# A transformer block on one core: the weight split of the seventh input chunk in halves and quarters, two small steps moved, and a new start address for the activations

## What is computed

```
hx = modulate(rmsnorm(x, norm1_g), mx[0], mx[1])       # mx = silu(c) @ ada_w + ada_b
hc = modulate(rmsnorm(ctx, norm1_g), mc[0], mc[1])     # mc = silu(c_ctx) @ ada_w + ada_b
ux = hx @ w_in
uc = hc @ w_in          # only the columns of the two forget gates and of the values are used
```

## Time and profile before

| | |
|---|---|
| median of 3 runs | 767.01 us |
| the profiled execution | 766.55 us |
| its span, first to last instruction | 764.7 us |
| PE busy | 738.8 us (97%) |
| DVE, ACT, POOL busy | 492.9, 360.9, 398.5 us |
| mean granted TensorE clock | 0.991 |

### The profile page before, as it was taken

One profiled execution on the slowest core, in us unless ns is written; L12 is line 12 of the kernel. 1 busy time (PEld: TensorE's weight loads), 2 busy tenths in 40 slices (PEclk: granted clock), 3 DMA queues, 4 the chain that ended last, 5 costly groups with the idle time before them and its releaser, 6 DMA issues.

```text
span 764.7 us, 14160 instructions
## 1 busy us (share of the span) xinstructions
PE 738.8 (97%) x5844; PEld 716.3 (94%) x5844; DVE 492.9 (64%) x905; ACT 360.9 (47%) x458; POOL 398.5 (52%) x223
## 2 busy tenths in 40 slices
PE   6887999999999989999999999999999999999998
PEld 3776889999999989999999999999999999999998
DVE  4886698369616559867777774457855656556553
ACT  6685333344434465555555546445554434334331
POOL 0775544347457957787887787766785300000000
PEclk9999999999999989999999999999999999999999
DMA  9993867436633546465554554443435564554511
GB/s 361 419 397 120 312 255 287 192 111 211 231 111 115 175 151 256 170 213 173 198 186 165 183 203 143 153 147 111 165 111 198 188 214 160 177 207 161 184 56 56
DMA packets 21089, 145.84 MB, mean 191 GB/s; under 512 B 2465, under 2 KB 2977, under 8 KB 3746
## 3 DMA queue, kind: packets, MB, share of 16 engines
q1 hardware_dynamic: 20880, 144.87, 52.0%
q10 hardware_dynamic: 146, 0.07, 0.0%
HBM read 143.88 MB, written 1.05 MB: 190 GB/s over the span
## 4 chain that ended last, share of the span: by engine, by line
PE 89%; DMA 3%; ACT 3%; DVE 2%; issue 1%; POOL 1%; DVEq 0%; ACTq 0%; POOLq 0%
PE bank L1433 24%; PE bank L1434 23%; PE bank L1435 23%; PE bank L1451 4%; DMA raw<-in_w_in 3%; PE CP L1435 2%; PE CP L1434 2%; PE CP L1433 2%; PE bank L1540 2%; POOL wlo L463 1%; ACT whi L490 1%; DVE GA L1136 1%; PE bank L1491 0%; PE CP L1465 0%; PE bank L1476 0%
## 5 line engine op out<-in xcount | busy, mean ns | idle before, releaser
L469 POOL TENSOR_TENSOR wlo<-raw,whi 128x512 fp32r<-128x512 f32 (+1 forms) x193 | 367.9, 1936 | 173.0 <-ACT whi L487 173.0
L487 ACT ACTIVATE whi<-raw 128x2048 fp32r<-128x2048 f32 x101 | 192.5, 1907 | 46.3 <-PE bank L1435 29.2
L1203 DVE SCALAR_TENSOR_TENSOR Y<-bank,vec,Y 128x189 f32<-128x189 f32 (+2 forms) x352 | 123.0, 423 | 43.8 <-ACT Y L738 43.8
L1433 PE MATMUL bank<-H2h,whi 128*128 128x256 f32 x352 | 100.0, 284 | 1.7 <-DVE H2l L1178 1.7
L1434 PE MATMUL bank<-H2l,whi 128*128 128x256 f32 x352 | 100.8, 286 | 0.0
L1435 PE MATMUL bank<-H2h,wlo 128*128 128x256 f32 x352 | 100.6, 286 | 0.0
L1433 PE MATMUL bank<-H1h,whi 128*128 128x256 f32 (+1 forms) x288 | 91.5, 318 | 9.0 <-ACT whi L487 5.7
L1435 PE MATMUL bank<-H1h,wlo 128*128 128x256 f32 (+1 forms) x288 | 89.7, 311 | 0.0
L1434 PE MATMUL bank<-H1l,whi 128*128 128x256 f32 (+1 forms) x288 | 89.4, 310 | 0.0
L863 DVE TENSOR_TENSOR wlo<-raw,whi 128x2048 fp32r<-128x2048 f32 x28 | 64.4, 2300 | 34.5 <-ACT whi L487 34.5
L1433 PE MATMUL bank<-H4h,whi 128*128 128x256 f32 x256 | 72.6, 283 | 0.0
(11 more groups left out here) (327 smaller groups left out, 1892.6 us busy)
## 6 DMA issues: line engine op xcount, KB each, us to landing
raw<-in_w_mlp SPq DMA_DIRECT2D x32, 1024.0 KB, 4.8
raw<-in_w_in SPq DMA_DIRECT2D x30, 1024.0 KB, 5.4
raw<-in_ffn_up SPq DMA_DIRECT2D x22, 1024.0 KB, 4.9
raw<-in_ada_hi SPq DMA_DIRECT2D x16, 1024.0 KB, 5.4
raw<-in_ffn_down SPq DMA_DIRECT2D x11, 1024.0 KB, 4.8
raw<-in_w_out SPq DMA_DIRECT2D x8, 1024.0 KB, 4.8
ada_s<-in_ada_s SPq DMA_DIRECT2D x4, 1024.0 KB, 17.7
ada_p<-in_ada_p SPq DMA_DIRECT2D x2, 1024.0 KB, 10.1
```

The source lines that it names most:

```text
L469: m = e.tensor_tensor(l[:, a:a + step], r[:, a:a + step], h[:, a:a + step].bitcast(F32), ALU.subtract)
L487: e.activation(whi[q % NHI][:, :], raw[n % NRAW][:, :], ACT.Copy).then_inc(s["w_hi"], 1)
L1203: e.scalar_tensor_tensor(o[:, r0:r1, c0:c1], z[:, r0 + dr:r1 + dr, c0 + dc:c1 + dc], cw[:, f, tap:tap + 1], o[:, r0:r1, c0:c1], ALU.mult, ...
L1433: e.matmul(out, h[:, col:col + P], xh, start=first, stop=False, skip_group_check=True)
```

## The change

- `FINE` is 7: chunk 6, the first forget chunk, is split in halves on ACT and in quarters on POOL like the chunks before it.
- ACT makes the two halves of chunk 6 earlier in its order: the first behind the context's tile 3, the second behind tile 5. Before, the whole chunk stood behind tile 7.
- DVE does the context's reciprocal behind the dot products of `ada_s` 2, not ahead of them.
- PE does all of chunk 3 and tiles 0 to 4 of chunk 4 ahead of the context's row products; tiles 5 to 7 of chunk 4 and chunk 5 follow them. For chunk 6 it waits half by half and quarter by quarter.
- The shared area begins at 124224 (the next multiple of 1024, plus 320), 352 bytes further on; modulo 1024 that is 320 instead of 992.

No instruction of computation is added but for one: chunk 6's one ACT copy becomes two of half the size. No DMA is added or moved.

```
-FINE = 6
+FINE = 7
...
-    base = cursor[0]
+    base = (cursor[0] + 1023) // 1024 * 1024 + 320
...
         input_high(1, range(2, 4))
+        first_high(6, 0)
         scales(1, 2, 22)
         input_high(1, (4, 5))
+        first_high(6, 1)
         scales(1, 3, 24)
         input_high(1, (6, 7))
-        high(6)
...
+        ada_rows("ada_s", 2, 1)
         reciprocal(2, 2, ("rms_in", 2), "rstd_in")
-        ada_rows("ada_s", 2, 1)
...
-        first(3, range(0, 5), b3)
+        first(3, range(0, 8), b3)
+        b4 = group("w_in", 4)
+        first(4, range(0, 5), b4)
         e.wait_ge(s["rstd_in"], 2)
         e.wait_ge(s["h1_mul"], 8)
         rows(bank[5][:, T:2 * T], [wide(2), wide(3)], "row_in")
-        first(3, range(5, 8), b3)
+        first(4, range(5, 8), b4)
+        first(5, range(0, 8), group("w_in", 5))
...
-            if i < 6:
-                first(i, range(0, 8), group("w_in", i))
-            elif i < 10:
-                h, l = weights("w_in", i)
+            if i < 10:
+                if i == 6:
+                    h, l = whi[i % NHI], wlo[i % NHI]
+                else:
+                    h, l = weights("w_in", i)
                 for j in range(2):
                     b = group("w_in", i, j)
                     for k in range(KT):
                         if (i, j) == (6, 0):
+                            e.wait_ge(s["w_hi"], hi_at[i] - 1 + k // 4)
+                            e.wait_ge(s["lo_pool"], 4 * i + k // 2 + 1)
```

More of the change, by code:

```diff
@@ L1584, in tensor @@
         hx, hl = H1h[:, 0, :, :], H1l[:, 0, :, :]
-        for i in range(4, 20):
-            if i < 6:
-                first(i, range(0, 8), group("w_in", i))
-            elif i < 10:
-                h, l = weights("w_in", i)
+        for i in range(6, 20):
+            if i < 10:
[3 more added lines that the diff above has]
+                    h, l = weights("w_in", i)
                 for j in range(2):
```

## The result

The kernel after takes **740.48 us** (median of 4 runs, 737.7 to 743.66) against 766.97 of the kernel before in the same rounds (4 runs, 766.56 to 767.05). The ratio is 0.966, with a 95% interval of 0.961 to 0.970. The two sets do not overlap; against the later one, with its own kernel before at 766.47, the gain is 20.2 us and not 26.5.

A forecast was written before the change was run, and what follows sets the result against it. PE bounds the kernel, busy 738.8 of 764.7 us. Order 2.85, wait 5.8, clock 1.45, less 0.6, give 9.5 us at chunk 6's end, 8.2 at chunk 7; address nothing: 758.8 us from 767.01, own range 757 to 760.5, overall 753.5 to 763.5.

The forecast's parts named there:

- The order around the row products and chunk 6 in halves: Steps at PE's early chunks: chunk 6 starts at 62.85, chunk 7 at 75.95 instead of 84.15, 8.2 us gained.
- 2.85 by the order, 5.8 by the wait: Split of the 9.5 us gained by chunk 6's end; 1.45 by the clock, less 0.6, complete it.
- The lead is kept: Chunks behind chunk 7: DVE and loads keep up, narrowest place 3.4 us at chunk 9, so the 8.2 us stay.
- Rival 1: Chunks 8 to 13: late DVE or raw-ring loads lose 2 to 6 of the 8.2 us, 761 to 765; chance 0.13.
- The clock at short waits: PE's waits of 0.6 us in chunk 6 and 1.2 us before chunk 7 leave the full clock.
- Rival 6: Clock falls at the wait before chunk 7: 1.45 us less gain, 760.2; chance 0.02.
- the rule of the Trainium skill: A matmul stream with waits can repeatedly drop to half clock; if chunk 7 began slow, gain 6.8 instead of 8.2 us.
- rival 2: Half clock behind 275 us, worth 2.6 us, shrinks or goes as waits move: 756.2 to 757.5; chance 0.12.
- The area's address: Every 256-column matmul streaming from the shared area: at most 12.8 us either way, taken as nothing.
- Rival 3: 256-column matmuls get faster by the area's address: up to 12.8 us more, 746 to 757; chance 0.11.
- the page that I named: Skill's SBUF page, Door 1: lines of 16 bytes, begun by both area positions, so the address price would be nothing.

The follow-up runs named there:

- order alone: Kernel after with the shared area back at 992 modulo 1024, so only the new order remains: 758.08 us, ratio 0.989.
- k1: Kernel after with the remainder of the fourth w_mlp1 chunk made by DVE instead of POOL: 735.31 us, ratio 0.960.
- k3: Kernel after unedited, run again later for the spread of its times: 746.25 us (745.3 to 750.75), ratio 0.976.
- halves alone: Kernel before with only chunk 6 in halves and quarters and its earlier place on ACT: 758.74 us, ratio 0.991.
- rows alone: Kernel before with only PE's new order around the row products and the later reciprocal: 767.00 us, ratio 1.0005.
- f3: Kernel after with the area at 128 modulo 1024, distance 0 from the weight tiles: slowest of all, 256-column matmuls at 120.0 ns.
- f4: Kernel after with the area at 448 modulo 1024, distance 320 from the weight tiles (64 modulo 256); total time not in the text.
- h1: Kernel after with the area at 992 and weight tiles at 800 modulo 1024, distance 192: fast; total time not in the text.
- h2: Kernel after with the area at 576 modulo 1024, distance 448 (192 modulo 256): profiled execution 746.88 us.
- h3: Kernel after with the area at 832 modulo 1024, distance 704 (192 modulo 512): profiled execution 740.38 us.
- g2: Kernel after with the area at 352 modulo 1024, 224 bytes from the weight tiles' residue; total time not in the text.
- f2: Kernel after with weight tiles at 192 and the area at 384 modulo 1024, distance 192 kept; total time not in the text.

## Why the prediction was right or wrong

**The order around the row products and chunk 6 in halves: right.** The trace of order alone (address as before) is the one to hold against the steps. Its ACT, POOL and PE:

```profile
58.62 1.05 ACT L490 ACTIVATE whi<-raw 128x1024 fp32r<-128x1024 f32 x1
...
68.22 0.60 ACT L587 ACTIVATE SG<-bank 128x512 f32<-128x512 f32 x1
68.72 1.91 ACT L487 ACTIVATE whi<-raw 128x2048 fp32r<-128x2048 f32 x1
```

```profile
62.55 2.55 POOL L463 TENSOR_TENSOR wlo<-raw,whi 128x512 fp32r<-128x512 f32 x2 [0.26 <-ACT whi L490]
70.70 10.04 POOL L469 TENSOR_TENSOR wlo<-raw,whi 128x512 fp32r<-128x512 f32 x8 [5.60 <-ACT whi L487]
```

```profile
54.49 0.61 PE L1440 MATMUL bank<-con,RC 128*128 128x128 f32 x4
...
62.87 0.39 PE L1434 MATMUL bank<-H1h,whi 128*128 128x512 f32 x1
...
68.87 0.50 PE L1434 MATMUL bank<-H1h,whi 128*128 128x512 f32 x1 [0.25 <-ACT SG L587]
...
75.84 0.47 PE L1434 MATMUL bank<-H1h,whi 128*128 128x512 f32 x1 [1.10 <-issue]
```

Row products without a wait, as forecast. Chunk 6 at 62.87 (forecast 62.85). Eviction done at 68.8 (69.0), PE's wait for it 0.25 us (0.6). `high(7)` at 68.72 (68.95). POOL's chunk 7 behind 70.7 (70.9). Wait before chunk 7 1.1 us (1.2), chunk 7 at 75.84 (75.95). Gain 84.15 - 75.84 = 8.3 us (8.2), and the median of the run gives the same 8.3.

**The split of that gain over its parts was misleading.** "2.85 by the order, 5.8 by the wait" adds up for the two together; with each alone it is 0.0 and 7.7.

**The lead is kept: right.** In the kernel with the order alone it is 8.2 to 8.35 at every n of the table. Rival 1 did not come.

**The clock at short waits: right where it was asked.** Behind 0.25 and 1.1 us in chunks 6 and 7 the matmuls of 512 columns keep 0.233 us. Rival 6 did not come, and the order's gain has no sign of the rule of the Trainium skill ("TensorE: Matmul & The Clock Gate", HAM oscillation) that I weighed against it. That short waits keep the clock is no rule, though: around the later wait of 2.4 us it fell, and behind one of 1.1 us it fell in k1 and k3 and stayed in the kernel after.

**Another clock phase behind 275 (rival 2): it moved and was worth 0.2 us.** In order alone the half clock lies at 267 to 274, no shorter than in the kernel before, and the lead goes from 8.1 to 8.3 us over it. The rival was real all the same: in halves alone and rows alone the half clock was half as long, and gave 1.1 and 1.3 us.

**The area's address: this is the step that failed.** The prediction put it as "If the position made that difference, the price would be 2.7 ns x 4752 = 12.8 us, either way ... I take nothing". Measured by itself it is 19.2 us (766.39 to 747.23). Two things in that step were wrong. The size of the term: the bound was taken from the nearest row, chunk 10 with whi as the streaming side, 117.3 ns, but that row is one distance (160) and the kernel after has another (192), with 113.3 ns, 6.7 ns less than before. At 4752 matmuls that would be 31.7 us; the kernel after is at 117.8 in one part and 113.3 in another, and pays 2.4 us of new wait and 1.6 us of clock. And the choice: chunk 10 showed that matmuls of the same count of columns and the same granted clock need not take 120.0 ns. I let the shape of the stream, two runs of 128, explain this as well, and it does not: with the same shape chunk 10 takes 120.0 ns in f3 and 113.3 in f4. "This trace has only one position for the tiles" was therefore a misreading. With the roles exchanged it had two distances, 96 and 160, and the 2.7 ns between them were the effect itself. Rival 3, which named the right mechanism, got 0.11, with a limit that the result passed by 5.5 us at its lower end (746).

**By the page that I named the price was nothing too.** The Trainium skill, "SBUF — State Buffer", says under Who interferes with whom that PE waits on nobody, and under Door 1 it knows lines of 16 bytes, at whose start all the tiles moved here begin. The runs differ from it: f3 and h1, which differ in these two addresses alone, are at 120.0 and at 113.3 ns over 320 to 380. The measurement decides.

**What stays open.** What in the chip makes the rate hang on the distance is not known; the runs show the dependence only. What draws 113.3 or 117.8 ns in a stretch at a distance of 192 (the feed-forward layer alone is 7.0 us, the MLP with its 1536 such matmuls 6.8). That this makes most of the scatter of the kernel after is argued, not shown: between the profiled executions of h2 and h3 it does, but the scatter within a kernel was not traced run by run. The profiled execution of k3 has the rates of that of the kernel after, so the step between the first four runs and the later five is not explained either; they were taken at another time, and whether the chip or the hour matters was not tried.

## What to carry to other kernels

When PE is the bound, read the time from start to start of its matmuls and compare kinds of one shape; if they differ at the same granted clock, try the start of the streamed tile against that of the stationary tile, here 192 modulo 256 bytes, before working on waits: it was worth more than twice the reordering. A term that the trace of before shows at one or two settings has no upper bound there; widen the range by it instead of taking nothing, and look first for rows that hold the same term at another value, as chunk 10 with its exchanged roles did here. When the bound engine gets faster, look again at the next engine: here POOL's one late chunk cost 4 us, and moving it to DVE gave them back.

## What the runs showed of the hardware

- The rate of fp32r matmuls with 128 x 128 weights and 256 streamed columns hangs on the distance from the start of the stationary to that of the streamed tile modulo 256 bytes, whichever of the two holds the weights: 120.0 ns at 0 and 96, 117.8 at 64, 118.7 at 128, 117.3 or 118.7 at 160, 113.3 or 117.8 at 192, 118.3 at 224, and 116.4 to 117.0 at 32 (g2, chunk 10). Matmuls of 512 columns take 226.7 ns at 0, 228.9 at 64 and 232.3 to 234.3 at the others.
- At 192 one stretch holds one of two rates, and it changed over a short break of PE (f2, x179 in 20 us and then x172).
- A GpSimd subtraction of a chunk took 8.00 us beside DVE instructions with two SBUF inputs (its last quarter alone 3.3 us), and 5.0 us at 70.12, where DVE did dot products with one input in SBUF and scalar operations.
- Waits of 0.25 to 1.1 us in chunks 6 and 7 left the granted clock at 1.00; behind 5.7 us it was 0.52, and over the stretch around the wait of 2.4 us it was 0.76. The same wait can go either way: behind 2.6 us it was 1.00 in the kernel before and 0.59 in halves alone, and behind 1.1 us 1.00 in the kernel after and 0.50 in k1.
